# First stage of a two-block transformer kernel: shift and scale loaded by halves of the features, and four projections split into two passes

## What is computed

```python
def modulation(c, w, b):
    return jnp.split(jax.nn.silu(c) @ w + b, 3, axis=-1)

def sandwich(x, mod, g_pre, g_post, fn):
    shift, scale, gate = mod
    h = rms_norm(x, g_pre) * (1.0 + scale[:, None]) + shift[:, None]
    return x + gate[:, None] * rms_norm(fn(h), g_post)

# first layer: fn projects h by hyb_w_in (1024 x 2560), whose column groups are
#   u (0:512) for a pooling over windows, q (512:1024), f (1024:1536), v (1536:2048), g (2048:2560)
# for a gated recurrence, then by hyb_w_out; after it come a feed-forward, an attention layer,
# another feed-forward, and the whole second block (fox/s5, experts, mLSTM, experts).
```

## Time and profile before

| | us |
|---|---|
| median of the runs | 1492.82 |
| profiled execution, whole | 1495.1 |
| its span in the profile | 1493.3 |
| end of the first stage's shift and scale | 34.2 |
| first matmul of piece 0 | 36.18 |
| first rescaling of the levels | 83.82 |

### The profile page before, as it was taken

How to read it: one execution, slowest core, us unless ns; L and a number is a source line. 1 busy time by engine, 2 the same in 40 slices (tenths; PEclk the granted TensorE clock), 3 DMA queues, 4 the chain that set the end, 5 groups by cost and what they waited for, 6 DMA issues and landing times.

```text
span 1493.3 us, 23591 instructions
## 1 busy us (share of the span) xinstructions
PE 1417.1 (95%) x9098; PEld 1263.4 (85%) x9098; DVE 1159.4 (78%) x1775; ACT 815.2 (55%) x1189; POOL 1.2 (0%) x5
## 2 busy tenths in 40 slices
PE   7989999999999999999999879999999999899997
PEld 7987899899998979999979768777879998787786
DVE  5998776876865656598569887799988966889997
ACT  2532433443443446444676436788866564678884
POOL 0000000000000000000000000000000000000000
PEclk8999999999999999999999999999999999999999
DMA  9983599986574614656635125899963534589992
GB/s 366 344 314 113 171 320 331 334 293 212 178 218 152 191 54 142 198 170 183 212 107 150 57 86 184 309 365 364 380 200 114 162 121 155 193 321 370 360 360 86
DMA packets 184483, 333.81 MB, mean 224 GB/s; under 512 B 13340, under 2 KB 127796, under 8 KB 184372
## 3 DMA queue, kind: packets, MB, share of 16 engines
q1 hardware_dynamic: 184372, 332.31, 64.7%
HBM read 331.18 MB, written 1.09 MB: 222 GB/s over the span
## 4 chain that ended last, share of the span: by engine, by line
PE 74%; DVE 14%; ACT 4%; DMA 4%; issue 3%; SPq 1%; ACTq 0%; DVEq 0%
PE PSA L634 15%; PE PSA L636 15%; PE PSA L635 15%; PE PSA L631 8%; PE PSB L634 5%; PE PSB L635 5%; PE PSB L636 5%; PE PSB L631 4%; DVE WL L1896 3%; DVE ACC L1893 2%; ACT WH L1405 1%; DVE T L1896 1%; DVE AR L1896 1%; DMA WR<-ffn_w_in 1%; DMA AD<-ada_w 1%
## 5 line engine op out<-in xcount | busy, mean ns | idle before, releaser
L1896 DVE TENSOR_TENSOR WL<-WR,WH 128x1024 fp32r<-128x1024 f32 x352 | 421.8, 1219 | 121.9 <-ACT WH L1405 121.1
L1405 ACT CAST WH<-WR 128x1024 fp32r<-128x1024 f32 x352 | 355.1, 1048 | 110.2 <-DMA WR<-hyb_w_in 44.4
L634 PE MATMUL PSA<-XH,WH 128*128 128x256 f32 x1312 | 380.3, 290 | 10.7 <-DVE WL L1896 2.9
L635 PE MATMUL PSA<-XL,WH 128*128 128x256 f32 x1312 | 373.3, 284 | 0.0
L636 PE MATMUL PSA<-XH,WL 128*128 128x256 f32 x1312 | 373.1, 284 | 0.0
L634 PEld LDWEIGHTS PSA<-XH,WH 128*128 128x128 f32 x1312 | 253.7, 193 | 17.2 <-issue 5.4
L635 PEld LDWEIGHTS PSA<-XL,WH 128*128 128x128 f32 x1312 | 254.0, 194 | 1.2 <-issue 0.7
L636 PEld LDWEIGHTS PSA<-XH,WL 128*128 128x128 f32 x1312 | 253.7, 193 | 0.0
L1896 DVE TENSOR_TENSOR WL<-AR,WH 128x1024 fp32r<-128x1024 f32 x152 | 178.3, 1218 | 19.2 <-ACT WH L1405 19.2
L634 PE MATMUL PSB<-WH,GH 128*128 128x512 f32 x416 | 165.1, 397 | 5.5 <-DVE GL L1896 5.5
L635 PE MATMUL PSB<-WL,GH 128*128 128x512 f32 x416 | 162.9, 392 | 0.0
(11 more groups left out here) (261 smaller groups left out, 2045.5 us busy)
## 6 DMA issues: line engine op xcount, KB each, us to landing
AR<-moe_w_gate_up SPq DMA_DIRECT2D x96, 512.0 KB, 5.7
WR<-ffn_w_in SPq DMA_DIRECT2D x88, 512.0 KB, 4.5
WR<-moe_w_gate_up SPq DMA_DIRECT2D x64, 512.0 KB, 5.7
AR<-ada_w SPq DMA_DIRECT2D x59, 512.0 KB, 8.8
AR<-moe_w_down SPq DMA_DIRECT2D x56, 512.0 KB, 6.0
WR<-ffn_w_out SPq DMA_DIRECT2D x44, 512.0 KB, 4.7
WR<-att_w_qkv SPq DMA_DIRECT2D x36, 512.0 KB, 4.7
AD<-ada_w SPq DMA_DIRECT2D x34, 512.0 KB, 5.8
```

The lines of the kernel that those rows point to most:

```text
L634: e.matmul(o, lh, rh, start=start, stop=False, skip_group_check=True)
L635: e.matmul(o, lh, rl, start=False, stop=False, skip_group_check=True)
L1405: A(e.copy(hi_slot(m), raw_slot(m)), s_hi)
L1896: return e.tensor_tensor(o, i, j, op)
```

## The change

**Blocks.** For x below 16, `load_ada` now brings 512 columns of shift and 512 of scale side by side: block k carries both for features 0 to 511 (the first half), block 8 + k both for features 512 to 1023. Each run in memory is 2048 bytes, where it was 4096. PE multiplies blocks 2, 5, 7 and 10, 13, 15 (six instead of four); DVE does the other ten (instead of twelve). Each half has a sum of its own, and `first_end(half)` finishes four shifts and four scales at once.

**Pieces.** The first eight pieces are reordered: 0 to 3 are the first halves (features 0 to 511) of u0, u1, q0, q1, and 4 to 7 their second halves. The four accumulations stay open between the sets. The first halves of u0, u1 and q0 run before the second half's sum, that of q1 behind it.

**Waits and loads.** SP interleaves pieces with blocks; pieces 4 to 7 are issued ahead of block 15 or right behind it, each behind its wait on `s_lo`. CT's rest comes after them. PR's rest moves to the start of the feed-forward, with a semaphore of its own (`s_late`). Blocks 16 to 23 hang behind pieces 5 to 9 instead of 1 to 8, and 24 to 27 behind pieces 13 and 14 instead of 12 and 13.

```diff
@@ weight_plan
-            cols("hyb_w_in", (0, 10))
+            for half in range(2):
+                for i in range(4):
+                    out.append(("hyb_w_in", "k", (0,), i * 256, half))
+            cols("hyb_w_in", (1024, 6))
@@ ada_plan, ada_places
-        pieces = {3: (12, 12, 13, 13, 16, 17, 17, 18), 4: (22, 22, 22, 22, 23, 24, 25, 26)}.get(p, range(at, at + 8))
+        pieces = {2: (5, 6, 7, 7, 8, 8, 9, 9), 3: (13, 13, 14, 14, 16, 17, 17, 18), 4: (22, 22, 22, 22, 23, 24, 25, 26)}.get(p) or range(at, at + 8)
-ADA_BY_PE = (12, 13, 14, 15)
+ADA_BY_PE = (2, 5, 7, 10, 13, 15)
@@ tensor
-            def half_of_features(u, half, stage):
+            def half_of_features(u, half, stage, first=None):
...
+            def first_rows(half, xs, opens=False, closes=False):
+                u = pring.uses["ada", half]
+                for x in xs:
+                    e.wait_ge(s_ada[ADA_PLACE[x]].sem, 16 * ADA_COUNT[x])
+                    for f in range(8):
+                        t = mm(bank(u.b, f, f + 1), ada_at[ADA_PLACE[x]][:, f * P:(f + 1) * P], csil[:, x % 8:x % 8 + 1],
+                               opens and x == xs[0] and f == 0, closes and f == 7, skip=True)
+                if closes:
+                    t.then_inc(u.fill[0], 1)
+            def first_sums(half):
+                u = pring.uses["ada", half]
+                e.wait_ge(s_adastep.sem, ada_count(8 * half + 7))
+                for f in range(8):
+                    mm(bank(u.b, f, f + 1), accs[half][:, f * P:(f + 1) * P], onesd[:, 0:1], False, False, skip=True)
+            def turn_first(half):
+                for j in range(4 * half, 4 * half + 4):
+                    if j % 2 == 0:
+                        u = use(("tp", 0, j), of=gring if half else ring, free=(s_t2.sem, j + 2))
+                    for m in range(2):
+                        t = mm(bank(u.b, j % 2 * 256 + m * P, j % 2 * 256 + m * P + P),
+                               XT[:, m * 1024 + j * P:m * 1024 + j * P + P], diag[:, m, :], True, True)
+                    if j % 2:
+                        t.then_inc(u.fill[0], 1)
+            def open_first(tag, at):
+                u = use(tag, fill=used(at + 4))
+                u.piece = at + 4
+                half_of_features(u, 0, "hyb", at == 0)
...
-            e.wait_ge(s_x.sem, 32)
-            busy(14)
...
+            busy(20)
+            e.wait_ge(s_csil.sem, 1)
+            for half in range(2):
+                use(("ada", half), of=pring)
+            first_rows(0, (2,), opens=True)
+            e.wait_ge(s_x.sem, 32)
+            e.wait_ge(s_diag.sem, 2)
+            turn_first(0)
+            first_rows(0, (5,))
+            busy(2)
+            first_sums(0)
+            busy(1)
+            first_rows(0, (7,), closes=True)
+            busy(2)
+            open_first(("u", 0), 0)
+            turn_first(1)
+            open_first(("u", 1), 1)
+            open_first(("q", 0), 2)
+            first_rows(1, (10, 13), opens=True)
+            first_sums(1)
+            first_rows(1, (15,), closes=True)
+            open_first(("q", 1), 3)
+            for tag in (("u", 0), ("u", 1), ("q", 0), ("q", 1)):
+                half_of_features(ring.uses[tag], 1, "hyb", tag == ("u", 0))
@@ scalar
-            pre(0)
+            for half in range(2):
+                hi_to(4 * half)
+                e.wait_ge(s_fscale.sem, half + 1)
+                for j in range(4 * half, 4 * half + 4):
...
+                    A(act(t2[:, j, :], bank(u.b, j % 2 * 256, j % 2 * 256 + 256), ACTF.Identity, bias=MC[:, j:j + 1],
+                          scale=MC[:, 8 + j:9 + j]), s_t2)
@@ vector
-            for x in range(4):
-                ada_step(x)
-            diagonals(rms(st_pre, 4))
-            for x in range(4, 12):
-                ada_step(x)
-            ada_end(0)
-            ada_end(1)
-            lo_to(0)
-            split_features(0)
...
+            def first_end(half):
+                u, js = pring.uses["ada", half], slice(4 * half, 4 * half + 4)
+                filled(u)
+                m = MC[:, 8 + 4 * half:12 + 4 * half]
+                V.frees(tt(v3(MC[:, 0:16], 2)[:, :, js], v3(bank(u.b, 0, 8), 2), v3(par("adab", 0, 16), 2)[:, :, js],
+                           ALU.add), u)
+                V.wait()
+                V(stt(m, m, 1.0, par("npre", 4 * half, 4), ALU.add, ALU.mult), s_fscale)
+            first_steps(0, 1)
+            diagonals(rms(st_pre, 4))
+            first_steps(3, 4, 6)
+            lo_to(0)
+            first_end(0)
+            split_features(0, 0, 4)
+            lo_to(1)
+            first_steps(8, 9)
+            lo_to(2)
+            first_steps(11, 12)
+            lo_to(3)
+            first_steps(14)
+            lo_to(4)
+            first_end(1)
+            split_features(0, 4, 8)
@@ sync
+                if x < 16:
+                    e.dma_start(v3(ada_at[i], 2), a["ada_w"][0, 0][k * P:(k + 1) * P, 0:2048].rearrange(
+                        "p (a h n) -> p h a n", a=2, h=2)[:, x // 8]).then_inc(s_ada[i].sem, 16)
+                    return
...
-            for x in ADA_FIRST:
+            raws = 0
+            for x in range(20):
                 load_ada(x)
...
+                if x in (6, 8, 10, 12, 14, 15):
+                    load_raw(raws)
+                    raws += 1
+                if x == 15:
+                    load_raw(6)
+                    load_raw(7)
+            e.dma_start(CT[:, EARLY_CONSTS:], a["consts"][:, EARLY_CONSTS:]).then_inc(s_rest.sem, 16)
...
-            for n in range(len(PLAN)):
+            for n in range(4, len(PLAN)):
...
+                    e.dma_start(PR[:, EARLY_PARAMS:], a["params"][:, EARLY_PARAMS:]).then_inc(s_late.sem, 16)
```

More of the change, by code:

```diff
@@ L227, in ada_places @@
         if x >= 20:
-            early = piece[x] - (9 if 24 <= x < 28 else 3 if 28 <= x < 32 else 8 if 32 <= x < 40 else 6)
+            early = 0 if x < 24 else piece[x] - (9 if 24 <= x < 28 else 3 if 28 <= x < 32 else 8 if 32 <= x < 40 else 6)
             if 22 <= i < 28:
                 early = max(early, FIRST["ffn", 0])
-            load.setdefault(max(early, piece.get(before[x], 0)), []).append(x)
+            load.setdefault(max(early, piece.get(before[x], 0), 4), []).append(x)
         last[i] = x
@@ L672, in piece @@
                 return n, hi_slot(n), lo_slot(n)
-            def half_of_features(u, half, stage):
+            def half_of_features(u, half, stage, first=None):
                 n, h, l = piece()
+                if first is None:
+                    first = n - FIRST[stage] < 2
                 h, l = v3(h, 4), v3(l, 4)
@@ L679, in half_of_features @@
                         kk = 4 * half + k
-                        if n - FIRST[stage] < 2 and f == 0:
+                        if first and f == 0:
                             e.wait_ge(s_xl.sem, 8 * SPLIT[stage] + kk + 1)
@@ L2014, in diagonals, with split_features @@
                     V(ts(diag[:, m, :], ident, y[:, m:m + 1], None, ALU.mult), s_diag)
-            def split_features(st):
+            def split_features(st, first=0, end=8):
                 at = [None] * 8
-                for j in range(8 + 1):
-                    if j < 8:
+                for j in range(first, end + 1):
+                    if j < end:
                         e.wait_ge(s_t2.sem, 8 * st + j + 1)
@@ L2023, in split_features @@
                     i = j - 1
-                    if i >= 0:
+                    if i >= first:
                         V.wait(at[i])
```

65 lines of the change are left out of this document (20 added, 45 removed).

## The result

The changed kernel takes **1507.97 us** (median of 4 runs, 1504.61 to 1510.32); the kernel before, beside it, 1492.22 (4 runs, 1490.6 to 1493.73). The ratio is 1.0085 with a 95% interval of 1.006 to 1.011: slower, by about 13 us (9 to 16). The two medians of four runs are 15.8 us apart, at the upper end of that interval; the later, longer series of the kernel before have medians of 1494.2 to 1496.2. The forecast of 1500 had the sign and the place, and was too small: 1507.97 lies above the range's upper end of 1505, and 1492.8 times 1.0085, which is 1505.5, just about on it. The profiled execution of the changed kernel is its slowest, 1510.3 with a span of 1508.5, which stands 15.2 above the span of before.

The account below looks back on a forecast made before the run. PE and DVE were both taken as close to full in the stage up to 84 us. First rescaling +4.9 and second level +2.6 gave +7.5 on the median 1492.8, so 1500 us, range 1492 to 1505.

Parts of the forecast that it names:

- PE up to F: Front on PE: F, the end of the second half's sum, comes at 49 us instead of 34.00.
- DVE from F: DVE's in-order work from the second half's sum to dif: 33.1 us against PE's 27; first rescaling 88.7, +4.9 us.
- SP and the transfers: Load queue: later issues cost nothing while 4 us of cover remain; without cover DVE's steps wait 1 to 3 us.
- Rival (d): Transfers late too: queue runs dry, blocks 20 to 23 late or second sum at 54; 1505 to 1508 us, chance 0.09.
- From dif to the first rescaling: PE's work from the pooling matmuls to the first rescaling: 6.6 us, as in the earlier trace.
- The second level: Blocks 26 and 27 now stand in it on DVE, whose work is the chain there: +2.6 us.
- (a): Rival: PE's clock stays full in the front, first rescaling 84.7; 1496 us, chance 0.14.
- (b): Rival: DVE keeps up, PE sets the stage, pooling matmuls at 76 or 74; 1490 or 1487 us, chance 0.10.
- (c): Rival: no change, second sum at 45 to 47, blocks 26 and 27 hidden; within 3 us of before, chance 0.09.

Follow-up runs that it names:

- e6: On top of e5, blocks 10 and 13 moved from PE to DVE; ratio 1.0020 to the kernel before.
- e12: Changed kernel with blocks 10 and 13 on DVE, piece 8 and blocks 20 to 22 issued on earlier waits, dif ahead of the decays; ratio 1.0015 to the kernel before.
- e3: Changed kernel with pooling weights and piece 8 issued after two splits, blocks 20 to 22 after the second sum; ratio 1.0061 to the kernel before.
- e5: Changed kernel with blocks 16 to 19 before the second sum, earlier-issued loads, dif before the decays, blocks 26, 27 before the first level; ratio 1.0013 to the kernel before.
- e8: Changed kernel with nine matmuls on constants on PE ahead of its wait for dif; ratio 1.0066 to the kernel before.
- e1: Changed kernel with blocks 26 and 27 behind piece 13 instead of 14, so ahead of the first level; ratio 1.0095 to the kernel before.
- b11: Kernel before with PE's early start on constants and the late load of PR's rest, without the halves; ratio 0.9999 to the kernel before.
- e7: Changed kernel with three matmuls on constants more on each side of the second half's sum; ratio 1.011 to the kernel before.

## Why the prediction held in sign and fell short in size

**PE up to F.** Nearly right. PE's start 3.2 (forecast 3.3), first half's end 27.2 (27), piece 0 at 29.4 (29), F 50.5 (49, ends 45 and 54). That 27 was met to 0.2 us is in part luck: the same PE instructions end at 24.2 in e6 and 27.5 in e12. The half clock was placed where it came, but it lasted from 21.8 to 32.0 and from 45.7 to 55.9, longer than the stretches that were taken from the earlier trace rows. Term: **+1.5 us**.

**DVE from F.** The list was right: 32.8 us in e3, where block 23 is not waited for, 33.1 forecast. PE's need of 27 us was put too low: in e5, whose list is shorter, PE is the bound with 28.9, and in the changed kernel PE reaches its wait at 83.7, 33.2 us behind F, so that it waits 3.8 us and not the 6 of the forecast. What failed is that the list was taken to run without waits. In the changed kernel 36.9 us pass from F to the end of `dif`, with 3.15 of wait for block 23 and 1.29 for ACT's sigmoids (0.30 in e3) among them. Against 33.1, term: **+3.8 us**.

**SP and the transfers, "I cost all this at nothing".** This step failed. The queue's wait for the eighth split was seen and the hole behind it named, but only piece 8 was followed through it; blocks 20 to 25 and pieces 8 to 11 come out of the same hole one after the other, and the last of them, block 23, is the one that is late. The price given for a lost cover, 1 to 3 us, was about right (3.15); it belonged into the sum. Rival (d) had this mechanism, with a chance of 0.09; its 1505 to 1508 holds the median, though the 2.9 us of the next term were not in it.

**From dif to the first rescaling, 6.6 us.** This step failed as well: 9.56 us, **+2.9**. The duration came from the earlier trace rows, where PE never paused ahead of it. In the forecast itself PE now waits 6 us at that place, and it knew from the earlier trace rows that this engine's clock falls; the two were not put together. e8 shows the 2.9 us as the clock's: filled up, the same wait costs 6.71.

The three make 8.2 of the 8.3 us that are missing at the first rescaling: 88.7 + 1.5 + 3.8 + 2.9 = 96.9 against 97.04 measured.

**The second level**, +2.6: right. From 97.04 to piece 15 the changed kernel takes 6.1 us, 3.5 before, and e1 gives it back in its trace. That nothing behind absorbs it held in this pair of traces (15.8 us at piece 15, 15.2 at the last remainder), but b11's trace lost its 2.8 us on the way, so the pair alone is weak evidence.

**Rivals.** (a) fell: the clock fell at 21.8 and 45.7, in the two places where the forecast had it, and at 76.4 and 86.7 besides. (b) fell because its condition, DVE's list below PE's, was not met; e5 meets it and still does not win, since F at 50.5 with PE's 28.9 behind it puts the pooling matmuls at 79.45, not at 76 or 74. The 27 us of nine pieces left out the sum of blocks 16 to 23 on PE, 16 one-column passes that take 1.92 us in the changed kernel (at 73.84), and the part of the pieces that runs at the half clock. (c), no change, fell with a ratio of 1.006 at the least.

**What stays open.** Why the clock falls at 45.7 with PE busy: e7 does not tell the one-column matmuls from other causes. The same for 76.4, which is in the changed kernel and not in e3. Whether a mended queue with a short front would win: e12 came to 1.0015 with block 23 still late, and no run moves blocks 24 and 25 behind it.

## What to carry to other kernels

A sum of durations across a stretch in which an engine newly waits must take that engine's clock into it: price the wait, and then the work behind the wait at the slower clock. When a queue waits for a late event, follow every transfer behind that wait to the instruction that reads it, above all the last one. Work pulled into an engine's idle time in front of a critical instruction must have its data there already, since an in-order engine will wait for it with the critical step behind.
